# A transformer block on one Trainium2 core: bank order and loads of the first down groups, and sums of squares taken tile by tile

## The chip, the cores and the metric

The kernel runs on one core of one Trainium2 chip. The metric is the device time of one execution in microseconds (us), taken over several runs; a separate execution was profiled, and all rows of a trace come from that one.

## The reference

One encoder block on 512 tokens of width 2048, in float32. Two groups of attention heads (8 grouped-query heads with 2 key/value heads, 8 latent-attention heads, 128 wide each) are each normalised and mapped back by one output projection; then comes a squared-ReLU MLP of width 8192.

```python
o = jnp.concatenate([rms_norm(o_a, g_out_a[l]), rms_norm(o_b, g_out_b[l])], axis=-1)
o = o @ w_out[l]
x = x + gt_a * rms_norm(o, g_post_attn[l])
h = rms_norm(x, g_pre_mlp[l]) * (1.0 + sc_m) + sh_m
y = jnp.square(jax.nn.relu(h @ w_mlp_in[l])) @ w_mlp_out[l]
x = x + gt_m * rms_norm(y, g_post_mlp[l])
```

`gt_a`, `sc_m`, `sh_m` and `gt_m` are parts of `silu(c) @ w_ada + b_ada`.

## The kernel before

Five engines run their own programs and wait on semaphores. Every large product is made three times at reduced precision: a float32 operand is split into a rounded half `hi` (ScalarE, ACT) and a rest `lo` (VectorE, DVE), and TensorE (PE) adds hi x hi, hi x lo and lo x hi in a PSUM bank. Split weights go through a ring of four slots (`RING`), one *unit* at a time: `hi_ready`, `raw_used` or `dn_lo`, and `w_used` count the units that ACT, DVE and PE are done with. SyncE (SP) issues nearly all loads in one order written out by hand, so a wait in SP holds back all loads that stand behind it.

**Output projection** (`out_block`, `out_unit`). Four column blocks of 8 units. A unit is 24 matmuls of 128x512: 4 token tiles `t` by 2 rows `q` by 3. Unit 0 of block 0 lies in the attention of the last head, so `out_block` begins with unit 1 there. The two groups of heads are normalised by their own sums of squares: POOL adds up the squares of each head into `sq_sum`, and `sum_squares` reduces these over the partitions by 12 one-column matmuls with a vector of ones (two instructions each, since they are plain float32) into 8 columns of bank 7. From `sq_reduced` DVE and ACT make `r_out`, which PE waits for ahead of unit 4 of the block (`r_ready`) and behind which ACT splits the weights of units 4 and on; those of units 1 to 3 are split earlier.

**Up stage** (`su_block`). 8 groups of 4 blocks, by a seven-product scheme in place of eight (`SLOTS`). It uses banks 4 to 7. Each block ends in a tile `y_out` that POOL saves to DRAM (`save_pair`, `y_ready`, `y_saved`). Between the blocks DVE adds a row of `w_ada` times a scalar to `gm_acc` (`gate_part`, from `gate_row`, which SP loads in `gate_behind`).

**Down stage** (`dn_products`, `dn_group`, `dn_loads`). 8 groups of rows of the weight, `g`; groups 0 to 6 run in two column halves `np`, and each (g, np) is seven products `i` of two units `h`, 14 units in all, again by the seven-product scheme. A unit is 12 matmuls of 128x512. Product `i` takes the values `y_use[k]`, with k = 0, 1, 2, 3, 4, 6, 5, and the block of weights 11, 12, 11, 22, 22-12 (`diff`), 21, 21, some of them mixed by DVE first (`third`, `one`, `two`, `four`). It writes a pair of banks given by `dn_banks`, and DVE adds the pair to `acc[i]` (`evict`, semaphore `evicted`). The order of DVE around the start of a (g, np) is `third(0)`, `unit_lo(0)`, `third(1)`, `unit_lo(1)`, `one(0)`, `one(1)`, `evict(before, 5)`, `unit_lo(2)`, `two(0)`, `unit_lo(3)`, `two(1)`, `evict(before, 6)`, `unit_lo(4)`. In (0, 0) the last steps of the up stage stand in this order too: behind `unit_lo(2)` comes the last `gate_part` and behind `unit_lo(6)` the last `pair_lo`, which makes `y_ready`.

PE waits for the banks of product i by

```python
wait_dn(pe, evicted, g, np, SLOTS, i - (1 if np == 0 and i < 2 else 2))
```

that is, in column half 0 product 0 waits until product 5 of the group before has been evicted, and product 1 until its product 6 has.

While (0, 1) runs, `spread_gm` multiplies the four column blocks of `gm_acc` by a matrix of ones, in banks 6 and 7, ACT copies each back (`gm_copied`), and POOL adds and multiplies two rows to each. The last group is done another way (`last_products`), 16 units in four column blocks over banks 0 to 3 and 4 to 7.

SP issues the loads at the seam in this order: weights 22, 11 and 12 of (0, 0); values 0 and 1; weights 21; `gate_row`; once the up stage is over values 2, 3 and 4; after `y_ready` values 6; after the last save (`y_saved`) values 5; then the weights 11, 12, 22 and 21 of (0, 1).

Of the kernel before, what the change touches and what calls it, by code (L numbers as in the profile page):

```python
# [26 lines left out]
P = 128  # L27
# [4 lines left out]
COLS = 512  # L32
# [159 lines left out]
def build(nc, a, out, x1_dram, y_dram):  # L192
    with ExitStack() as ctx:
# [336 lines left out]
            return (a_11, s, s, a_12, a_21, a_12, a_22[i % 2])[e]  # L530

        def dn_banks(np, i):
            return 2 * ((SLOTS * np + i) % 3)

        def last_at(n, t):

# [8 lines left out]
        def _(sp):  # L545
# [114 lines left out]
            def gate_behind(g, i):  # L660

                k = 2 * g + (i // 2) if isinstance(g, int) else g * 2 + (i // 2)
                issue = gate_load(k, i % 2)
                if isinstance(g, int) and su_count(g, i, 1) == 0:
                    sp.wait_ge(y_done, 2 * SU_FIRST)
                else:
                    sp.wait_ge(gate_used, su_count(g, i, 1))
                issue()
# [58 lines left out]
            weights(0, 0, "11")  # L727
            weights(0, 0, "12")
            sp.wait_ge(w_used, SU_W + end + 3)
            sp.wait_ge(y_saved, 16 * PAIRS)  # L730
            values(0, 0)
            values(0, 1)
# [1 line left out]
            weights(0, 0, "21", (0,))  # L734
            sp.wait_ge(su_lo, end + 6)
            weights(0, 0, "21", (1,))
            gate_behind(LAST, PAIRS - 1)
            sp.wait_ge(w_used, DN_W)
            for k in (2, 3, 4):
                values(0, k)  # L740
            sp.wait_ge(y_ready, GROUPS * PAIRS)
            values(0, 6)
            sp.wait_ge(y_saved, 16 * GROUPS * PAIRS)
            values(0, 5)
            weights(0, 1, "11")

            def dn_loads(g, np, behind=True):

                def free(n):
                    return lambda: wait_dn(sp, dn_lo, g, np, DN_UNITS, n)  # L750

                def next_values(i):
                    if np:
                        values(g + 1, PRODUCTS[i][1], lambda: sp.wait_ge(w_used, at_dn(g, np, 2 * i + 1).count(1, 1)))

                to = (g + 1, 0) if np else (g, 1)
                weights(*to, "12", free=free(4))
                weights(*to, "22", free=free(8))
                next_values(0)
                next_values(1)  # L760
                next_values(2)
                next_values(3)
                weights(*to, "21", free=free(DN_UNITS))
                if behind:
                    weights(g + 1, np, "11")
                    for i in range(4, SLOTS):
                        next_values(i)
# [3 lines left out]
                n, u = divmod(j, PAIRS)  # L771
                sp.dma_start(last_w[j % LAST_RING][:], w_dn_last[LAST * PAIRS + u, :, :, n * COLS:(n + 1) * COLS]).then_inc(last_landed[j % LAST_RING], 16)

            with sp.Fori(0, LAST - 1) as g:
                dn_loads(g, 0)
                dn_loads(g, 1)
            dn_loads(LAST - 1, 0, behind=False)
# [66 lines left out]
        def _(act):  # L844
# [546 lines left out]
            def final_root(t):  # L1391
                act.wait_ge(y_var, t + 1)
                nc.scalar.activation(stat_s[:, t, 2:3], stat_v[:, t, 2:3], ACT.Sqrt).then_inc(y_sqrt, 1)

            act.wait_ge(x1_saved, 16 * NT)
            plain_blocks()
            su_groups(act, su_block)

            for u in range(2, DN_UNITS):
                unit_hi(0, 0, u)  # L1400
                if u == 2:
                    square_rest(LAST, PAIRS - 1)
                if u == 5:
                    pair_hi(LAST, PAIRS - 1)
            for u in range(DN_UNITS):
                unit_hi(0, 1, u)
                if u >= 7 and u % 2:
                    n = (u - 7) // 2
                    act.wait_ge(gm_reduced, n + 1)
                    nc.scalar.activation(gm_acc[:, n * COLS:(n + 1) * COLS], bank[6 + n % 2][:], ACT.Copy).then_inc(gm_copied, 1)  # L1410
            with act.Fori(1, LAST) as g:
                for np in range(2):
                    for u in range(DN_UNITS):
# [14 lines left out]
        def _(dve):  # L1428
# [868 lines left out]
            def last_evict(n):  # L2297

                dve.wait_ge(w_used, LAST_W + PAIRS * (n + 1))
                for th in range(2):  # L2300
                    b = 4 * (1 - n % 2) + 2 * th
                    dst = acc[((6, 1), (5, 3))[th][n % 2]][:, n // 2, :, :]
                    tt(dst, psum[:, b:b + 2, :], dst, ALU.add).then_inc(last_evicted, 1)

# [8 lines left out]
            def last_tile_sum(t):  # L2313

                dve.wait_ge(last_tile, t + 1)
                y = last_at(NB - 1, t)
                tt(y, bank[t][:], y, ALU.add).then_inc(last_evicted, 1)
                dve.wait_ge(last_evicted, 2 * (NB - 1) + t + 1)
                tt(z_last[:, t, :], y, gm_acc[:, (NB - 1) * COLS:NB * COLS], ALU.mult).then_inc(z_ready, 1)

# [49 lines left out]
        def _(pe):  # L2370
# [280 lines left out]
            def out_unit(n, j, only=range(NT)):  # L2651

                unit_tokens(at_out(n, j)[1], sets[j // 4], o_hi, o_lo, QROWS * out_rows(j), j % 4 == 0, j % 4 == 3, only=only)
# [56 lines left out]
            attend(2 * HEADS - 1, None, stage["v"], HEADS)  # L2710


            def sum_squares():

                pe.wait_ge(sq_ready, 2 * HEADS - 1)
                pe.wait_ge(pt_done, 4 * 2 * HEADS)
                pe.wait_ge(o_done, 2 * HEADS)
                for g in range(2):
                    for t in range(NT):
                        c = 16 + 4 * g + t  # L2720
                        tile = slice(t * P, (t + 1) * P)
                        ins = mm(bank[7][:, c:c + 1], sq_sum[:, g, tile], ones[:, 0:1], start=True, stop=g == 0)
                        if g:
                            ins = mm(bank[7][:, c:c + 1], sq[:, tile], ones[:, 0:1], start=False, stop=True)
                ins.then_inc(sq_reduced, 1)

            def spread_ga(n):

# [5 lines left out]
            def out_block(n, first=False):  # L2734

                for j in range(1 if first else 0, UNITS_D):
                    wait_out(n, j)
                    out_unit(n, j)
                    if j == 1 and first:
                        sum_squares()  # L2740
                    if j == 6:
                        spread_ga(n)

# [121 lines left out]
            def dn_products(g, np, behind=lambda i: None, ahead=lambda i: None):  # L2865

                for i in range(SLOTS):
                    k = PRODUCTS[i][1]
                    b = dn_banks(np, i)
                    ahead(i)  # L2870
                    if np == 0:
                        pe.wait_ge(y_landed[k], g * 16 + 16)
                    wait_dn(pe, evicted, g, np, SLOTS, i - (1 if np == 0 and i < 2 else 2))
                    for h in range(2):
                        w = at_dn(g, np, 2 * i + h)
                        wait_dn(pe, dn_lo, g, np, DN_UNITS, 2 * i + h + 1)
                        s = w.slot()
                        for m in range(2):
                            for q in range(QROWS):
                                j = 2 * h + q  # L2880
                                yh, yl = (y_use[k][:, j, x, m * P:(m + 1) * P] for x in range(2))
                                mm(bank[b + m][:], yh, hi[s][:, q, :], start=j == 0, stop=False)  # L2882
                                mm(bank[b + m][:], yh, lo[s][:, q, :], start=False, stop=False)  # L2883
                                ins = mm(bank[b + m][:], yl, hi[s][:, q, :], start=False, stop=j == PAIRS - 1)  # L2884
                        ins.then_inc(w_used, 1)
                    behind(i)
# [21 lines left out]
            def free_banks(i):  # L2908
# [3 lines left out]
                if i == 2:  # L2912
                    pe.wait_ge(su_c, 3 * SU_BLOCKS)

            def spread_gm(i):

                n = i - 1
                if n == 0:
                    pe.wait_ge(gate_used, SU_BLOCKS)
                    pe.wait_ge(su_x, SU_BLOCKS)  # L2920
                if 0 <= n < NB:
                    if n >= 2:
                        pe.wait_ge(gm_copied, n - 1)
                    mm(bank[6 + n % 2][:], ones[:], gm_acc[:, n * COLS:(n + 1) * COLS], start=True, stop=True).then_inc(gm_reduced, 1)

            dn_products(0, 0, ahead=free_banks)
            dn_products(0, 1, behind=spread_gm)
            with pe.Fori(1, LAST) as g:
                for np in range(2):
                    dn_products(g, np)  # L2930
# [1 line left out]
            def last_products(n, j, t):  # L2932

                s = At(LAST_W + n * PAIRS + j).slot()
                b = 4 * (1 - n % 2) + t
                for q in range(QROWS):
                    yh, yl = (y_use[2 * q + t // 2][:, j, x, (t % 2) * P:(t % 2 + 1) * P] for x in range(2))
                    mm(bank[b][:], yh, hi[s][:, q, :], start=j == 0 and q == 0, stop=False)
                    mm(bank[b][:], yh, lo[s][:, q, :], start=False, stop=False)  # L2939
                    ins = mm(bank[b][:], yl, hi[s][:, q, :], start=False, stop=j == PAIRS - 1 and q == QROWS - 1)  # L2940
                return ins
# [188 lines left out]
```

## Time and profile before

| | |
|---|---|
| runs before | 2078.06 us median of 3 (2077.61 to 2078.45) |
| time of the profiled execution | 2083.07 us |
| its span | 2081.4 us |
| granted TensorE clock, mean over the span | 0.989 |
| PE busy | 2024.3 us (97% of the span) |
| DVE busy | 1717.5 us (83%) |
| ACT busy | 992.1 us (48%) |
| out-projection, from the squares' sums to unit 3 of block 0 | 577.55 to 588.88 us |
| (0, 0) and (0, 1) of the down stage | 1426.56 to 1520.27 us |
| (1, 0) to (6, 1) of the down stage | 1520.27 to 1985.34 us |

Times within a trace count from the start of its span. PE matmuls are pipelined, so the distance from one start to the next, and not the length of a row, is what a matmul costs. The granted clock is the share of TensorE's full clock: 1.00 is 2.4 GHz and 0.50 is 1.2 GHz.

### The profile page before, as it was taken

What the parts mean: (1) busy time and instruction counts of PE and PEld (TensorE: products, weight loads), DVE (VectorE), ACT (ScalarE), POOL (GpSimd) and SP (SyncE); (2) the same over time, 40 slices, a digit from 0 to 9 for tenths busy, and PEclk for the clock granted to TensorE, in tenths of its full rate; (3) what the DMA queues carried; (4) which work ended last, traced back from release to release, by engine and by line L of the source; (5) the groups of instructions that cost most, each with busy time, mean ns of one, the idle gap of its engine ahead of it and who ended that gap; (6) DMA issues with size and microseconds to landing.
All of it is one profiled execution on the core that took longest, in us unless ns stands there. A gap on an engine that the chain in (4) does not pass through costs nothing.

```text
span 2081.4 us, 30860 instructions
## 1 busy us (share of the span) xinstructions
PE 2024.3 (97%) x11186; PEld 1762.0 (85%) x11186; DVE 1717.5 (83%) x2013; ACT 992.1 (48%) x1403; POOL 155.1 (7%) x163
## 2 busy tenths in 40 slices
PE   6999999999999989999999999999999999999998
PEld 6787888878888868899999999998778888888886
DVE  5986898778877777699999999987788888888866
ACT  4454322578833264455565655654333333333322
POOL 0000000057600000000000000000020000000000
PEclk8999999999999999999999999999999999999999
DMA  8996869610186744766667666677756446446452
GB/s 295 344 303 220 280 204 253 200 46 1 54 296 227 241 161 129 247 210 220 224 217 232 212 229 212 218 245 283 258 209 242 181 182 243 181 181 249 174 182 81
DMA packets 296285, 435.37 MB, mean 209 GB/s; under 512 B 30180, under 2 KB 180360, under 8 KB 287368
## 3 DMA queue, kind: packets, MB, share of 16 engines
q1 hardware_dynamic: 278056, 361.43, 52.4%
q0 software_dynamic: 16704, 67.11, 8.8%
q10 hardware_dynamic: 1440, 5.70, 0.8%
q8 instruction: 53, 0.87, 0.2%
q14 instruction: 32, 0.26, 0.0%
HBM read 367.09 MB, written 67.11 MB: 209 GB/s over the span
## 4 chain that ended last, share of the span: by engine, by line
PE 81%; DVE 8%; DMA 4%; issue 3%; ACT 3%; SPq 1%; DVEq 0%; ACTq 0%
PE bank L2860 8%; PE bank L2862 8%; PE bank L2861 8%; PE bank L2882 7%; PE bank L2884 7%; PE bank L2883 7%; PE bank L2384 6%; PE bank L2385 6%; PE bank L2386 6%; PE bank L2397 2%; PE bank L2399 2%; PE bank L2398 2%; DMA raw<-in_w_ada 1%; PE bank L2940 1%; PE bank L2939 1%
## 5 line engine op out<-in xcount | busy, mean ns | idle before, releaser
L2882 PE MATMUL bank<-hi,y_use 128*128 128x512 f32 x784 | 310.2, 396 | 13.9 <-DVE lo L2200 8.5
L1375 ACT ACTIVATE hi<-w 128x1024 fp32r<-128x1024 f32 x168 | 178.1, 1062 | 296.1 <-PE bank L2884 219.9
L2883 PE MATMUL bank<-lo,y_use 128*128 128x512 f32 x784 | 306.6, 391 | 0.0
L2884 PE MATMUL bank<-hi,y_use 128*128 128x512 f32 x784 | 306.6, 391 | 0.0
L851 ACT ACTIVATE hi<-raw 128x1024 fp32r<-128x1024 f32 (+2 forms) x132 | 128.9, 992 | 275.9 <-PE bank L2386 99.6
L1294 ACT ACTIVATE hi<-a 128x1024 fp32r<-128x1024 f32 x182 | 191.9, 1054 | 142.9 <-DVE a L2088 130.4
L2085 DVE TENSOR_TENSOR lo<-a,hi 128x1024 fp32r<-128x1024 f32 x182 | 221.9, 1219 | 40.9 <-ACT hi L1294 40.5
L2200 DVE TENSOR_TENSOR lo<-w,hi 128x1024 fp32r<-128x1024 f32 x168 | 205.2, 1226 | 38.7 <-ACT hi L1375 37.3
L2860 PE MATMUL bank<-h_hi,hi 128*128 128x256 f32 x832 | 235.6, 283 | 0.7 <-DVE c_b L2115 0.7
L2861 PE MATMUL bank<-h_lo,hi 128*128 128x256 f32 x832 | 235.5, 283 | 0.0
L2862 PE MATMUL bank<-h_hi,lo 128*128 128x256 f32 x832 | 235.4, 283 | 0.0
L1436 DVE TENSOR_TENSOR lo<-raw,hi 128x1024 fp32r<-128x1024 f32 (+2 forms) x130 | 147.5, 1141 | 91.8 <-ACT hi L851 89.6
L2882 PEld LDWEIGHTS bank<-hi,y_use 128*128 128x128 f32 x784 | 148.2, 189 | 51.3 <-issue 15.4
L2883 PEld LDWEIGHTS bank<-lo,y_use 128*128 128x128 f32 x784 | 148.3, 189 | 31.3 <-issue 1.0
L2884 PEld LDWEIGHTS bank<-hi,y_use 128*128 128x128 f32 x784 | 148.1, 189 | 31.1
L2860 PEld LDWEIGHTS bank<-h_hi,hi 128*128 128x128 f32 x832 | 159.7, 192 | 0.9 <-DVE c_b L2115 0.9
L2861 PEld LDWEIGHTS bank<-h_lo,hi 128*128 128x128 f32 x832 | 159.7, 192 | 0.0
L2862 PEld LDWEIGHTS bank<-h_hi,lo 128*128 128x128 f32 x832 | 159.7, 192 | 0.0
L2384 PE MATMUL bank<-hi,h_hi 128*128 128x512 f32 x320 | 125.9, 393 | 1.9 <-ACT q_o L1009 1.4
L2088 DVE TENSOR_TENSOR a<-a,a 128x1024 f32<-128x1024 f32 x104 | 124.9, 1221 | 2.4 <-DMA a<-in_w_mlp_in 0.6
L2386 PE MATMUL bank<-hi,h_lo 128*128 128x512 f32 x320 | 124.6, 389 | 0.0
L2385 PE MATMUL bank<-lo,h_hi 128*128 128x512 f32 x320 | 124.6, 389 | 0.0
(384 smaller groups left out, 4715.8 us busy)
## 6 DMA issues: line engine op xcount, KB each, us to landing
raw<-in_w_ada SPq DMA_DIRECT2D x166, 512.0 KB, 5.1
w<-in_w_mlp_out SPq DMA_DIRECT2D x128, 512.0 KB, 4.8
y_dram<-y_out POOLq DMA_DIRECT2D x32, 1792.0 KB, 6.8
y_use<-y_dram SPq DMA_DIRECT2D x53, 1024.0 KB, 9.0
a<-in_w_mlp_in SPq DMA_DIRECT2D x104, 512.0 KB, 4.5
raw<-in_w_in SPq DMA_DIRECT2D x32, 512.0 KB, 5.7
raw<-in_w_out SPq DMA_DIRECT2D x32, 512.0 KB, 4.8
gate_row<-in_w_ada SPq DMA_DIRECT2D x26, 512.0 KB, 5.1
```

The costliest lines, as they stand in the source:

```text
L1294: nc.scalar.activation(hi[w.slot()][:], su_weight(i, e)[:].rearrange("p (q k) n -> p q (k n)", q=QROWS), ACT.Copy).then_inc(hi_ready, 1)
L2085: tt(lo[w.slot()][:], src, hi[w.slot()][:].bitcast(F32), ALU.subtract).then_inc(su_lo, 1)
L2200: tt(lo[w.slot()][:], weight(np, i, h)[:], hi[w.slot()][:].bitcast(F32), ALU.subtract).then_inc(dn_lo, 1)
L2384: mm(acc[t][:], xh, hi[s][:, q, :], start=first and q == 0, stop=False)
L2385: mm(acc[t][:], xh, lo[s][:, q, :], start=False, stop=False)
L2386: ins = mm(acc[t][:], xl, hi[s][:, q, :], start=False, stop=last and q == QROWS - 1)
L2860: mm(into[e], wh, bh, start=opens and k == 0, stop=False, skip_group_check=not opens)
L2861: mm(into[e], wh, bl, start=False, stop=False, skip_group_check=not opens)
L2862: ins = mm(into[e], wl, bh, start=False, stop=k == KH - 1, skip_group_check=not opens)
L2882: mm(bank[b + m][:], yh, hi[s][:, q, :], start=j == 0, stop=False)
L2883: mm(bank[b + m][:], yh, lo[s][:, q, :], start=False, stop=False)
L2884: ins = mm(bank[b + m][:], yl, hi[s][:, q, :], start=False, stop=j == PAIRS - 1)
```

## The change

1. `dn_banks` gives the 14 products of a group four pairs of banks in place of three, in the order 0 1 2 0 1 2 0 | 1 2 3 0 1 2 3, and the wait for evictions is `i - 2` everywhere. The last group's blocks use the other half of the banks (`4 * (n % 2)`).
2. `spread_gm` moves from (0, 1) to (0, 0), behind products 3 to 6, and its copies on ACT move with it; (0, 1) waits for them ahead of product 2.
3. SP loads `gate_row` ahead of values 0 and 1, and the weights 11, 12 and 22 of (0, 1) ahead of values 6 and 5. The first round of `dn_loads` is written out ahead of the loop.
4. `sum_squares` is cut into four parts of 3 matmuls (6 instructions), one for each token tile. They stand behind tiles 2 and 3 of unit 1 and behind tiles 0 and 1 of unit 2.

```diff
         def dn_banks(np, i):
-            return 2 * ((SLOTS * np + i) % 3)
+            return 2 * (0, 1, 2, 0, 1, 2, 0, 1, 2, 3, 0, 1, 2, 3)[SLOTS * np + i]
...
             sp.wait_ge(w_used, SU_W + end + 3)
+            gate_behind(LAST, PAIRS - 1)
             sp.wait_ge(y_saved, 16 * PAIRS)
             values(0, 0)
             values(0, 1)
...
             weights(0, 0, "21", (1,))
-            gate_behind(LAST, PAIRS - 1)
             sp.wait_ge(w_used, DN_W)
             for k in (2, 3, 4):
                 values(0, k)
+            sp.wait_ge(y_done, 2 * GROUPS * PAIRS - 1)
+            weights(0, 1, "11")
+            weights(0, 1, "12", free=lambda: sp.wait_ge(dn_lo, 4))
             sp.wait_ge(y_ready, GROUPS * PAIRS)
             values(0, 6)
+            weights(0, 1, "22", free=lambda: sp.wait_ge(dn_lo, 8))
             sp.wait_ge(y_saved, 16 * GROUPS * PAIRS)
             values(0, 5)
-            weights(0, 1, "11")
...
-                weights(*to, "12", free=free(4))
-                weights(*to, "22", free=free(8))
+                if not begun:
+                    weights(*to, "12", free=free(4))
+                    weights(*to, "22", free=free(8))
...
-            with sp.Fori(0, LAST - 1) as g:
+            dn_loads(0, 0, begun=True)
+            dn_loads(0, 1)
+            with sp.Fori(1, LAST - 1) as g:
...
+                if u in (10, 12):
+                    gate_copy((u - 10) // 2)
             for u in range(DN_UNITS):
                 unit_hi(0, 1, u)
-                if u >= 7 and u % 2:
-                    n = (u - 7) // 2
-                    act.wait_ge(gm_reduced, n + 1)
-                    nc.scalar.activation(gm_acc[:, n * COLS:(n + 1) * COLS], bank[6 + n % 2][:], ACT.Copy).then_inc(gm_copied, 1)
+                if u in (0, 2):
+                    gate_copy(u // 2 + 2)
...
-            def sum_squares():
+            def sum_squares(t):
...
                 for g in range(2):
-                    for t in range(NT):
-                        c = 16 + 4 * g + t
...
+                    c = 16 + 4 * g + t
...
+                if t == NT - 1:
+                    ins.then_inc(sq_reduced, 1)
...
-                    out_unit(n, j)
-                    if j == 1 and first:
-                        sum_squares()
+                    if first and j in (1, 2):
+                        for t in range(NT):
+                            out_unit(n, j, only=(t,))
+                            if j == 1 and t >= 2 or j == 2 and t < 2:
+                                sum_squares(t - 2 if j == 1 else t + 2)
+                    else:
+                        out_unit(n, j)
...
-                    wait_dn(pe, evicted, g, np, SLOTS, i - (1 if np == 0 and i < 2 else 2))
+                    wait_dn(pe, evicted, g, np, SLOTS, i - 2)
...
+            def free_gate_banks(i):
+
+                if i == 2:
+                    pe.wait_ge(gm_copied, NB)
...
-                n = i - 1
+                n = i - 3
...
-            dn_products(0, 0, ahead=free_banks)
-            dn_products(0, 1, behind=spread_gm)
+            dn_products(0, 0, behind=spread_gm, ahead=free_banks)
+            dn_products(0, 1, ahead=free_gate_banks)
...
-                b = 4 * (1 - n % 2) + t
+                b = 4 * (n % 2) + t
```

## Rows read from the trace of the kernel before

**Rows 1.** The page's first part: busy time, share of the span, instructions.
```profile
PE 2024.3 (97%) x11186; PEld 1762.0 (85%) x11186; DVE 1717.5 (83%) x2013; ACT 992.1 (48%) x1403; POOL 155.1 (7%) x163
```

**Rows 2.** PE's waits over the span: total us, times, longest.
```profile
PE bank L2882 <- DVE acc L2280: 3.8, 5, 0.8
```

**Rows 3.** Timeline of PE, down stage: start, length, instruction, [idle before <- releaser].
```profile
1426.56 0.47 PE L2882 MATMUL bank<-hi,y_use 128*128 128x512 f32 x1
...
1434.58 0.39 PE L2884 MATMUL bank<-hi,y_use 128*128 128x512 f32 x1
1439.98 0.80 PE L2882 MATMUL bank<-hi,y_use 128*128 128x512 f32 x1 [5.01 <-DVE lo L2200]
...
1443.66 0.40 PE L2882 MATMUL bank<-hi,y_use 128*128 128x512 f32 x1
...
1475.26 0.77 PE L2882 MATMUL bank<-hi,y_use 128*128 128x512 f32 x1 [3.52 <-DVE lo L2200]
...
1480.52 0.53 PE L2882 MATMUL bank<-hi,y_use 128*128 128x512 f32 x1
...
1489.28 0.80 PE L2882 MATMUL bank<-hi,y_use 128*128 128x512 f32 x1
...
1495.63 0.80 PE L2882 MATMUL bank<-hi,y_use 128*128 128x512 f32 x1
...
1985.34 0.39 PE L2938 MATMUL bank<-hi,y_use 128*128 128x512 f32 x1
```

**Rows 4.** Timeline of DVE at the first two down groups.
```profile
1436.37 1.28 DVE L2123 SCALAR_TENSOR_TENSOR gm_acc<-gate_row,silu_c,gm_acc 128x1024 f32<-128x1024 f32 x1 [5.39 <-DMA gate_row<-in_w_ada]
...
1472.75 1.23 DVE L2204 TENSOR_TENSOR diff<-w,w 128x1024 f32<-128x1024 f32 x1 [8.40 <-issue]
```

**Rows 5.** Timelines of SP's and POOL's queues: values 0, values 2, last save.
```profile
1416.15 0.40 SPq L717 DMA_DIRECT2D y_use<-y_dram  x1
...
1426.47 0.34 SPq L717 DMA_DIRECT2D y_use<-y_dram  x1
...
1447.23 0.94 POOL L3068 DMA_DIRECT2D y_dram<-y_out  x1 [27.25 <-DVE y_out L2042]
```

**Rows 6.** DMA issues, us to landing: values 0, 2, 5; the last saves but one, and last.
```profile
y_use<-y_dram SPq DMA_DIRECT2D x1, 1024.0 KB, 10.3
...
y_use<-y_dram SPq DMA_DIRECT2D x1, 1024.0 KB, 12.4
...
y_use<-y_dram SPq DMA_DIRECT2D x1, 1024.0 KB, 5.0
...
y_dram<-y_out POOLq DMA_DIRECT2D x1, 1792.0 KB, 14.5
...
y_dram<-y_out POOLq DMA_DIRECT2D x1, 1792.0 KB, 10.6
```

**Rows 7.** Windows of 20 us: busy time by engine, PEclk, DMA share, GB/s.
```profile
1420.00:1440.00 20.00, 14.87 (x91) 12.94 (x89) 12.60 (x13) 7.44 (x10) 0.00 (x0) 1.00 1.03 415
```

**Rows 8.** Timeline of PE where groups 3 and 4 begin.
```profile
1674.84 0.39 PE L2884 MATMUL bank<-hi,y_use 128*128 128x512 f32 x1
1675.99 0.49 PE L2882 MATMUL bank<-hi,y_use 128*128 128x512 f32 x1 [0.76 <-DVE acc L2280]
...
1753.56 0.49 PE L2882 MATMUL bank<-hi,y_use 128*128 128x512 f32 x1 [0.77 <-DVE acc L2280]
```

**Rows 9.** Timeline of DVE where group 3 begins.
```profile
1678.05 1.22 DVE L2200 TENSOR_TENSOR lo<-w,hi 128x1024 fp32r<-128x1024 f32 x1
```

**Rows 10.** Timeline of PE around the sums of squares, and a like burst later.
```profile
577.55 1.17 PE L2722 MATMUL bank<-ones,sq_sum 128*128 128x1 f32 x10
...
580.57 0.77 PE L2384 MATMUL bank<-hi,o_hi 128*128 128x512 f32 x1
...
588.88 0.39 PE L2384 MATMUL bank<-hi,o_hi 128*128 128x512 f32 x1
...
734.79 1.84 PE L2770 MATMUL bank<-ones,mod_acc 128*128 128x1 f32 x16
```

More of the change, by code:

```diff
@@ L740, in _, with dn_loads @@
                 values(0, k)
+            sp.wait_ge(y_done, 2 * GROUPS * PAIRS - 1)
+            weights(0, 1, "11")
+            weights(0, 1, "12", free=lambda: sp.wait_ge(dn_lo, 4))
             sp.wait_ge(y_ready, GROUPS * PAIRS)
             values(0, 6)
+            weights(0, 1, "22", free=lambda: sp.wait_ge(dn_lo, 8))
             sp.wait_ge(y_saved, 16 * GROUPS * PAIRS)
             values(0, 5)
-            weights(0, 1, "11")
-            def dn_loads(g, np, behind=True):
+            def dn_loads(g, np, behind=True, begun=False):
                 def free(n):
@@ L1393, in final_root, with gate_copy @@
                 nc.scalar.activation(stat_s[:, t, 2:3], stat_v[:, t, 2:3], ACT.Sqrt).then_inc(y_sqrt, 1)
+            def gate_copy(n):
+                act.wait_ge(gm_reduced, n + 1)
+                nc.scalar.activation(gm_acc[:, n * COLS:(n + 1) * COLS], bank[6 + n % 2][:], ACT.Copy).then_inc(gm_copied, 1)
             act.wait_ge(x1_saved, 16 * NT)
@@ L2300, in last_evict @@
                 for th in range(2):
-                    b = 4 * (1 - n % 2) + 2 * th
+                    b = 4 * (n % 2) + 2 * th
                     dst = acc[((6, 1), (5, 3))[th][n % 2]][:, n // 2, :, :]
@@ L2316, in last_tile_sum @@
                 y = last_at(NB - 1, t)
-                tt(y, bank[t][:], y, ALU.add).then_inc(last_evicted, 1)
+                tt(y, bank[4 + t][:], y, ALU.add).then_inc(last_evicted, 1)
                 dve.wait_ge(last_evicted, 2 * (NB - 1) + t + 1)
@@ L2710, in _ @@
             attend(2 * HEADS - 1, None, stage["v"], HEADS)
-            def sum_squares():
-                pe.wait_ge(sq_ready, 2 * HEADS - 1)
-                pe.wait_ge(pt_done, 4 * 2 * HEADS)
-                pe.wait_ge(o_done, 2 * HEADS)
-                for g in range(2):
-                    for t in range(NT):
-                        c = 16 + 4 * g + t
[L2721 to L2725, printed above, removed]
+            def sum_squares(t):
+                if t == 0:
+                    pe.wait_ge(sq_ready, 2 * HEADS - 1)
+                    pe.wait_ge(pt_done, 4 * 2 * HEADS)
+                    pe.wait_ge(o_done, 2 * HEADS)
+                for g in range(2):
+                    c = 16 + 4 * g + t
+                    tile = slice(t * P, (t + 1) * P)
+                    ins = mm(bank[7][:, c:c + 1], sq_sum[:, g, tile], ones[:, 0:1], start=True, stop=g == 0)
+                    if g:
+                        ins = mm(bank[7][:, c:c + 1], sq[:, tile], ones[:, 0:1], start=False, stop=True)
+                if t == NT - 1:
+                    ins.then_inc(sq_reduced, 1)
             def spread_ga(n):
@@ L2920, in spread_gm @@
                     pe.wait_ge(su_x, SU_BLOCKS)
-                if 0 <= n < NB:
+                if n >= 0:
                     if n >= 2:
```

## The prediction

> **What bounds the kernel now.** First the page's busy times: PE works 97% of the span [rows 1]. So time is to be had only where PE stands still or runs at half clock. I then went through PE's waits by stage. Two stretches are touched by the change.
>
> In the down stage the timeline of PE shows a matmul every 0.227 us (from 1426.56 to 1434.58 there are 35 steps in 8.02 us, of which the first is 0.08 longer than the others), so a unit of 12 takes 2.72 us [rows 3]. From 1426.56 to 1985.34 there are 14 x 14 = 196 units, which would fill 533.1 us; the stage took 558.8. The four gate matmuls explain part of the difference: between the units behind two of them lie 6.35 us in place of 5.44, so 0.91 each, 3.6 in all [rows 3]. The rest is 558.8 - 533.1 - 3.6 = **22.1 us** of standstill and slow clock. It lies in three places:
>
> - PE stops after three units, at 1434.58, and goes on at 1439.98: 5.2 us beyond the usual step. Then nine steps take until 1443.66, 3.7 in place of 2.0: 1.6 lost at half clock [rows 3]. DVE shows why: its last gate_part waited 5.39 us for gate_row, until 1436.37, and two(0) and unit_lo(3) stand behind it in its program [rows 4].
> - PE stops for 3.52 us (3.7 in steps) before 1475.26, the start of (0, 1); then twelve steps take until 1480.52, 5.3 in place of 2.7: 2.5 lost [rows 3]. DVE idled 8.40 us until 1472.75 ahead of third(0), which needs weights 12 and 22 of (0, 1) [rows 4]. SP issued them only after the last save and values 5.
> - At the six starts of groups 1 to 6 PE waits for an eviction [rows 2, 8]. The step there is 1.15 us in place of 0.23, and from one start to the next 77.57 us pass in place of 28 x 2.72 = 76.16: 1.4 each [rows 8]. Six make 8.5, and with the first two places that is 21.5; the last 0.6 is at the seam of groups 0 and 1, where both waits are longer.
>
> In the output projection the squares' sums begin at 577.55, unit 2 at 580.57 and unit 3 at 588.88 [rows 10]. So the sums take 3.0 us, and the 24 matmuls behind them 8.3 in place of 5.44, because the clock fell to its lower level after some 2 us of one-column matmuls.
>
> **The change part by part.**
>
> *Bank order and `i - 2`.* Nothing is added. With four pairs, product 0 of a group waits for product 4 of the one before instead of 5, and product 1 for 5 instead of 6. DVE evicts product 4 even before third(0), so both waits at a group's start go: 8.5 + 0.6 = 9.1 us. What is late next? DVE's run at the start is long: from unit_lo(13) to unit_lo(4) it has 15 operations of 1.1 to 1.2 us with no idle time. Its unit_lo(3) begins at 1678.05 and ends at 1679.3 [rows 9]. PE, started at 1674.84 + 0.23 = 1675.07, wants unit 3 at 1683.2, and the eviction of product 6 (ready at about 1681.5) with product 2 at 1685.9. The slack is 3.9 and 4.4 us, so I take the whole 9.1. Bounds: 7 to 9.1.
>
> *Gate row first.* It is issued at about 1416.2, where values 0 were [rows 5], so it is there long before DVE wants it at 1431, and gate_part costs its 1.28 us and no wait. DVE's chain moves up by 5.39 us, unit_lo(3) is ready at 1439.98 - 5.39 = 1434.6, and PE wants it at 1434.8. Both the 5.2 and the 1.6 us go. But the row's 0.52 MB now stand ahead of values 0, which landed at 1416.15 + 10.3 = 1426.45, just as PE began at 1426.56 [rows 5, 6]: that load is critical already. In that stretch the DMA moved 415 GB/s [rows 7], so 0.52 MB cost 1.3 us; if a save that lands in 14.5 us takes its 127 GB/s of that [rows 6], 1.8. And values 2, whose place in the queue is unchanged in bytes, land at 1426.47 + 12.4 = 1438.9 [rows 5, 6]; PE wants them with unit 4, at 1426.56 + 4 x 2.72 = 1437.4. The old stall hid that. The two delays don't add, since the first moves the second's demand: unit 4 begins at the later of 1437.4 + 1.3 to 1.8 and 1438.9, so at about 1439.0. **New loss 1.6** (bounds 1.5 to 2.7).
>
> *Weights of (0, 1) earlier.* 11 is issued at about 1428, 12 at unit_lo(3), 1434.5, and 22 at unit_lo(7), near 1442.5. Six loads of 0.52 MB behind values 4 are 3.1 MB, or 7.6 us of the DMA. All land by 1457, while third(0) of (0, 1) comes up at about 1460: the 3.7 and 2.5 us go. What is late next is values 6 and 5. y_ready comes 5.4 us earlier, so the last save starts at 1447.23 - 5.4 = 1441.8 [rows 5], but now against a full queue. It took 10.6 us with one load beside it, and the one before 14.5 with a full queue [rows 6]: it lands at 1452.4 to 1456.3. Values 5 take 5.0 more [rows 6], 1457.4 to 1461.3. PE wants them with unit 12: 1439.0 + 8 x 2.72 + 3 x 0.91 = 1463.5. Values 6 (in the queue behind 11 and 12) land near 1455, wanted at 1457.1. So no stall, by a slack of 2 us.
>
> *Gate matmuls in (0, 0).* The same four, 3.6 us as before, moved. Each copy on ACT now waits up to a unit for its matmul, so unit_hi(11), (13), (15) and (17) start about a microsecond after PE leaves the unit whose slot they take. PE wants them three units, 8.2 us, later; hi and lo need 2.3. Cost nothing. POOL's rows move up 40 us and nobody waits for them before the last group.
>
> *Written-out round, banks of the last group.* Same instructions, same waits: nothing.
>
> *Squares tile by tile.* The 24 small instructions stay, 0.107 us each: 2.6 us, and PE pays some 0.1 to get going again after each part, four times in place of once: 3.0 in all. No part is longer than 0.7 us, between stretches of 1.36 us of full matmuls. A burst of 16 such instructions took 1.84 us at 734.79 and the clock stayed at 1.00 [rows 10]; so I expect it to stay here. From 577.55 to unit 3 it was 11.3 us; it becomes 5.44 + 3.0 = 8.4: **2.9 saved** (bounds: 0 or a loss of 0.3, to 2.9). `sq_reduced` comes at 583.2 instead of 580.6. Behind it on DVE and ACT stand the square root and the splits of units 4 and on; unit_lo(4) moves from 584.1 to about 586.5, and PE wants it at 586.0 + 5.4 = 591.4. Hidden.
>
> **Sum.** 22.1 - 1.6 + 2.9 = 23.4 us. From the profiled execution's 2083.07 us that gives 2059.7 (span 2058.0). The median of the runs, 2078.06, is 5.0 lower than the profiled time; it holds the same waits, though perhaps less of them, so I take 23.0 from it: **2055.1 us**.
>
> **Rivals.**
>
> *A. A late load keeps a stall.* The slack of values 5 and 6 is 2 us and rests on how save and loads share the DMA; the first stall (values 0) may be 2.7 us. For: the DMA is full from 1414 to 1442. Against: the old stall was no busier. With a stall of 1 to 3 us and a slow clock behind it (1.6 to 2.5 [rows 3]), it loses 3 to 5 more: 2058 to 2060.
>
> *B. The clock falls anyway.* The one-column parts now alternate with full matmuls over some 6 us, and the clock could fall after any of them. Then the 2.9 are not saved and the additional starts cost 0.3: 2055.1 + 3.2 = 2058.3. Against it stand the burst at 734.79 and the standstills of 0.8 at the groups' starts, which all left the clock at 1.00 [rows 8, 10]. The Trainium skill (TensorE: Matmul & The Clock Gate, HAM oscillation) says that where bursts of matmuls are divided by waits, the clock can fall again at every burst; by that rule spreading could cost more than one block does. The trace bears the rule out for standstills of 3.5 and 5.0 us, and not for short ones.
>
> *C. The bank order does not do what it says.* If another thing of DVE's run is just behind the eviction, the six starts keep their 1.4: 2064. Against: 3.9 us of slack.
>
> *D. Slower than before.* Place: the same run of DVE at the six group starts. If it slipped, PE would stop at unit 3 instead. To eat all 23 us, each start must lose 3.9, so the run must be 3.9 + 3.9 = 7.8 us later than now; that needs each of its 15 operations to take 0.5 longer, 1.7 in place of 1.2 [rows 9]. Nothing in the change lengthens them beyond POOL's eight operations on gm_acc, which lie elsewhere.
>
> **How the numbers follow.** The forecast has 60%, A 20%, B 11%, C 5%, D 2%; 2% is for what I haven't seen, both ways. The range reaches from 2053.0 (no new loss at values 0 and 2, and the last half microsecond of the sum) to 2061.5 (A and B together, less than C). Faster by over 0.2% (4 us, about what a measurement can tell from none): 96%; within it 2%; slower 2%.
>
> **What would show it.** In the trace after: PE goes on at 1434.6 without a stop (times less 2.9 for the projection); DVE's gate_part has no wait; a stop of about 1.5 us in all at values 0 and 2; no stop at the start of (0, 1); no wait for an eviction; 76.2 us from group to group; one-column rows in four parts at full clock. It would be wrong if PE shows a stop of over 2 us anywhere in (0, 0), if unit_lo appears as PE's releaser at the group starts, or if the clock is below 1.00 anywhere from 575 to 590.

## The result and the profile after

| | before | changed |
|---|---|---|
| median of the runs on one chip | 2078.26 us (2077.61 to 2083.28, 4 runs) | 2061.22 us (2057.57 to 2067.83, 4 runs) |
| ratio, 95% interval | | 0.992 [0.9903, 0.9937] |
| profiled execution, its span | 2083.07, 2081.4 us | 2067.83, 2066.1 us |
| mean granted clock in it | 0.989 | 0.989 |

The change makes the kernel faster by 17.0 us between the medians, 16.6 us by the ratio. The forecast was 23.0 us, to 2055.1 us. The median lies inside the range, 0.3 us below its upper end.

The page of the changed kernel has the same instructions as [rows 1], and PE is less busy by 4.7 us:

```profile
PE 2019.6 (98%) x11186; PEld 1762.8 (85%) x11186; DVE 1720.7 (83%) x2013; ACT 992.2 (48%) x1403; POOL 154.8 (7%) x163
```

PE's waits over the span, changed kernel (total us, times, longest). The row of [rows 2] has no counterpart. What is new is a wait in front of a down matmul (L2898) and a longer wait for `lo` in the projection (L2775). `issue` means that the profile names no releaser:

```profile
PE bank L2649 <- DVE pt_lo L1820: 5.2, 6, 1.4
PE bank L2793 <- DVE z_tok L2019: 3.5, 1, 3.5
...
PE bank L2898 <- issue: 2.1, 1, 2.1
PE bank L2775 <- DVE lo L1447: 1.9, 1, 1.9
```

The timeline of PE in the down stage, the answer to [rows 3]. The first rows are the first down unit; 1474.57 is the start of (0, 1), with the last gate matmuls in front of it. Neither the stop behind unit 2 nor the one at (0, 1) is left. The new stop stands in front of the first unit:

```profile
1431.58 0.47 PE L2898 MATMUL bank<-hi,y_use 128*128 128x512 f32 x1 [2.09 <-issue]
...
1432.51 0.63 PE L2898 MATMUL bank<-hi,y_use 128*128 128x512 f32 x1
...
1435.07 0.63 PE L2898 MATMUL bank<-hi,y_use 128*128 128x512 f32 x1
1435.49 0.44 PE L2899 MATMUL bank<-lo,y_use 128*128 128x512 f32 x1
...
1474.12 1.02 PE L2945 MATMUL bank<-gm_acc,ones 128*128 128x512 f32 x2
1474.57 0.80 PE L2898 MATMUL bank<-hi,y_use 128*128 128x512 f32 x1
...
1513.10 0.39 PE L2898 MATMUL bank<-hi,y_use 128*128 128x512 f32 x1
...
1589.26 0.39 PE L2898 MATMUL bank<-hi,y_use 128*128 128x512 f32 x1
...
1970.06 0.39 PE L2959 MATMUL bank<-hi,y_use 128*128 128x512 f32 x1
```

From 1431.58 to 1435.49 there are 10 steps, which take 3.91 us in place of 2.35: the clock was at half for a while. The stop ends with values 0. Their load is issued at 1419.38 and takes 12.1 us in place of the 10.3 in [rows 6], so it lands at 1431.5, and PE goes on at 1431.58:

```profile
y_use<-y_dram SPq DMA_DIRECT2D x1, 1024.0 KB, 12.1
```

1513.10 and 1589.26 are the starts of groups 1 and 2, 76.16 us apart, as 28 units of 2.72 are. DVE's last `gate_part` follows straight on the operation ahead of it, in place of the wait of 5.39 us in [rows 4]:

```profile
1433.94 1.28 DVE L2134 SCALAR_TENSOR_TENSOR gm_acc<-gate_row,silu_c,gm_acc 128x1024 f32<-128x1024 f32 x1
```

SP's queue at the seam (the counterpart of [rows 5]): the gate's row, values 0 and 1, then behind the up stage values 2 to 4, the weights of (0, 1), values 6 and values 5:

```profile
1419.00 0.34 SPq L658 DMA_DIRECT2D gate_row<-in_w_ada  x1
1419.38 0.93 SPq L717 DMA_DIRECT2D y_use<-y_dram  x2
...
1429.52 1.40 SPq L717 DMA_DIRECT2D y_use<-y_dram  x3
1430.97 7.83 SPq L710 DMA_DIRECT2D w<-in_w_mlp_out  x4
1445.23 0.34 SPq L717 DMA_DIRECT2D y_use<-y_dram  x1
...
1458.72 0.34 SPq L717 DMA_DIRECT2D y_use<-y_dram  x1
```

The timeline of PE at the sums of squares, now in four parts (the first two are shown), and at the burst of 16 that [rows 10] has at 734.79:

```profile
576.61 0.50 PE L2733 MATMUL bank<-ones,sq_sum 128*128 128x1 f32 x4
576.98 0.36 PE L2735 MATMUL bank<-ones,sq 128*128 128x1 f32 x2
577.20 0.48 PE L2395 MATMUL bank<-hi,o_hi 128*128 128x512 f32 x1
...
578.67 0.50 PE L2733 MATMUL bank<-ones,sq_sum 128*128 128x1 f32 x4
...
586.19 0.39 PE L2395 MATMUL bank<-hi,o_hi 128*128 128x512 f32 x1
...
731.07 0.50 PE L2775 MATMUL bank<-hi,o_hi 128*128 128x512 f32 x1 [1.93 <-DVE lo L1447]
...
734.37 3.41 PE L2786 MATMUL bank<-ones,mod_acc 128*128 128x1 f32 x16
```

586.19 is the start of unit 3. In the last projection block PE waits 1.93 us for unit 7, and the same burst of 16 then takes 3.41 us in place of 1.84. Windows over the two places tell why. The third number from the end is PE's granted clock, the last two are the DMA's share and GB/s. First the kernel before, then the changed one:

```profile
576.00:592.00 16.00, 16.00 (x70) 13.53 (x69) 10.81 (x17) 7.49 (x10) 1.59 (x3) 0.79 0.91 341
730.00:746.00 16.00, 15.41 (x75) 12.38 (x74) 11.82 (x22) 9.25 (x18) 0.00 (x0) 1.00 0.56 201
```

```profile
576.00:592.00 16.00, 16.00 (x84) 13.65 (x83) 11.33 (x18) 6.98 (x10) 1.60 (x3) 1.00 0.78 291
730.00:746.00 16.00, 14.93 (x50) 11.92 (x51) 8.32 (x13) 5.22 (x11) 0.00 (x0) 0.68 0.47 172
```

The fall of the clock at the sums is gone, and one that costs some 5 us stands behind the wait for unit 7: a mean of 0.68 over 16 us.

To compare all kernels I read the starts of PE's instructions at the borders of three stretches: from the last matmul of the attention to the first transpose of `z_tok` (the projection); from the last matmul of the up stage to the start of (1, 0) (the seam); from there to the last group (groups 1 to 6). From the start of the last group to PE's last matmul it is 86.8 us in each. `Unit 7` is PE's wait for it in the last projection block.

| traced kernel | projection | unit 7 | seam | groups 1 to 6 |
|---|---|---|---|---|
| before, first trace | 182.2 | 0.6 | 94.1 | 465.1 |
| before, again | 180.4 | 1.9 | 93.0 | 464.5 |
| changed, first trace | 185.4 | 1.9 | 83.9 | 457.0 |
| changed, again | 185.6 | 2.2 | 81.8 | 457.0 |
| changed, sums in one block | 183.1 | 2.3 | 82.5 | 457.0 |
| changed, values 0 first | 179.3 | 0.8 | 82.4 | 457.0 |
| before, sums by tiles | 185.9 | 2.3 | 93.6 | 465.3 |
| before, new loads | 178.7 | 0.2 | 82.8 | 464.3 |
| before, new banks | 179.5 | 1.0 | 94.0 | 457.0 |
| values 0 first, unit 4 early | 178.2 | 0 | 82.1 | 457.0 |
| the same, again | 178.2 | 0 | 81.6 | 457.0 |
| the same, sums in one block | 178.2 | 0 | 81.8 | 457.0 |
| before, unit 4 early | 178.2 | 0 | 92.9 | 464.4 |

### The profile page after: what moved, and what is told of

Its sections match the earlier page's. It is cut to its first block, busy times and chain, and to the rows that moved or that the text cites. A ratio compares the mean times of both kernels' runs of the same rounds, so it can differ in the third digit from the quotient of the medians.

```text
span 2066.1 us, 30799 instructions
## 1 busy us (share of the span) xinstructions
PE 2019.6 (98%) x11186; PEld 1762.8 (85%) x11186; DVE 1720.7 (83%) x2013; ACT 992.2 (48%) x1403; POOL 154.8 (7%) x163
## 4 chain that ended last, share of the span: by engine, by line
PE 82%; DVE 6%; DMA 5%; ACT 3%; issue 3%; SPq 0%; DVEq 0%; ACTq 0%
PE bank L2898 9%; PE bank L2900 9%; PE bank L2899 9%; PE bank L2876 8%; PE bank L2877 8%; PE bank L2878 8%; PE bank L2395 4%; PE bank L2397 4%; PE bank L2396 4%; DMA raw<-in_w_out 2%; DMA raw<-in_w_ada 2%; PE bank L2408 2%; PE bank L2410 2%; PE bank L2409 2%; PE bank L2961 1%
## 5 line engine op out<-in xcount | busy, mean ns | idle before, releaser
L2898 PE MATMUL bank<-hi,y_use 128*128 128x512 f32 x784 | 307.7, 393 | 2.1 <-issue 2.1
L1447 DVE TENSOR_TENSOR lo<-raw,hi 128x1024 fp32r<-128x1024 f32 (+2 forms) x130 | 147.6, 1143 | 84.7 <-ACT hi L857 82.1
L2898 PEld LDWEIGHTS bank<-hi,y_use 128*128 128x128 f32 x784 | 147.7, 188 | 33.6 <-issue 3.2
```

## The experiments

Two theories stood at the start. **Theory 1**: the down stage gives what was forecast, and what is missing is the clock of single executions and a later wait in the projection. **Theory 2**: one of the parts costs time of its own, the sums by tiles above all. The first four kernels ran together on one chip, so did the later ones in their groups. Ratios are against the kernel before on the same chip.

**The change again, timed in more runs.** No edit.

> The changed kernel again, for its spread. Four runs of it lie between 2057.6 and 2067.8 us and their mean granted clocks between 0.995 and 0.989. Theory 1, the spread is the clock: in every run the span times the mean clock is the same within 2 us (2043 to 2046 in those four), and the best runs, at 0.995, take about 2057. Theory 2, the spread is in waits for loads: runs of the same clock differ by more than 3 us.

Measured: 2061.36 us (2054.39 to 2064.69, 6 runs), ratio 0.9914 [0.99, 0.9928]. The gain repeats, and so does the gap to the forecast. The runs are 10 us apart, and their mean clocks go from 0.996 (2054.39 us) to 0.992 (2064.69 us). A span times its clock stays within 2043.7 to 2046.5, so most of the spread between runs is the clock; the 2.8 us that stay are a little over the 2 us expected (the clock's third digit is worth 1 us either way). The trace has the wait for unit 7 (2.2 us) with a clock of 0.68 from 730 to 746 again, but a stop of only 1.10 us ahead of the first down unit and no clock fall behind it. Here PE also waits a little ahead of unit 4, for values 2, which land at 1440.87:

```profile
1440.96 0.47 PE L2898 MATMUL bank<-hi,y_use 128*128 128x512 f32 x1 [0.25 <-issue]
```

**The sums in one block, the rest as changed.** `sum_squares` is the whole one again too.

```diff
...
-                    if first and j in (1, 2):
...
-                    else:
-                        out_unit(n, j)
+                    out_unit(n, j)
+                    if j == 1 and first:
+                        sum_squares()
```

> The change with the squares' sums in one block again. If the tile-by-tile sums save their 2.9 us to the end, this is 2.9 slower than the change. If the gain is lost again in the last block of the output projection, where PE now waits 1.9 us for a split weight in place of 0.6 and the clock falls behind it, this is as fast as the change or faster, and its trace shows 0.6 us there and a clock of 1.00 from 732 to 744.

Measured: 2060.9 us (2057.93 to 2065.56, 6 runs), ratio 0.9921 [0.9908, 0.9934]. The medians are 0.5 us apart, not 2.9. But the sign that I had named for a gain lost again, a wait of 0.6 us and a clock of 1.00 there, isn't in the trace either. Its windows show something else: no fall at the sums (1.00), though they are in one block, and a shorter one behind the wait for unit 7 (0.89), which is 2.3 us.

```profile
576.00:592.00 16.00, 16.00 (x85) 13.64 (x84) 11.59 (x18) 7.07 (x10) 1.59 (x3) 1.00 0.89 321
730.00:746.00 16.00, 15.99 (x69) 12.70 (x70) 11.34 (x21) 7.62 (x16) 0.00 (x0) 0.89 0.45 158
```

**Values 0 ahead of the gate's row in SP's queue.**

```diff
-            gate_behind(LAST, PAIRS - 1)
             sp.wait_ge(y_saved, 16 * PAIRS)
             values(0, 0)
+            gate_behind(LAST, PAIRS - 1)
             values(0, 1)
```

> The gate row's load is issued behind values 0 and ahead of values 1. If the 2.1 us stop at the start of the down stage is the 0.5 MB ahead of values 0, the stop goes, so does the slow clock behind it, and what is left is a wait of about 1.5 us for values 2: 0.7 us faster than the change by the stops alone, up to 2.7 with the clock. If values 2 are not what is late next, 2.1 to 4.1 us faster. DVE's gate_part still has no wait by either.

Measured: 2058.71 us (2057.96 to 2059.14, 5 runs), ratio 0.9911 [0.9898, 0.9924]. The stop ahead of the first unit is 0.74 us. A second one of 0.74 is for values 1, which now stand behind the gate's row and land at 1428.81, and one of 0.19 for values 2 follows; all leave the clock at 1.00.

```profile
1428.85 0.50 PE L2898 MATMUL bank<-hi,y_use 128*128 128x512 f32 x1 [0.74 <-DMA y_use<-y_dram]
```

That is 1.7 us of stops in all, where the traces of the change have 2.1 and 1.4: the loss has moved to the next load. The median is 2.6 us lower than that of the change, but the ratios' intervals lie over each other and the seam is no shorter in the table (82.4 against 81.8). So a gain from this order is not shown.

**The sums by tiles alone, on the kernel before.** The diff's part 4.

```diff
...
-                    out_unit(n, j)
-                    if j == 1 and first:
-                        sum_squares()
+                    if first and j in (1, 2):
+                        for t in range(NT):
+                            out_unit(n, j, only=(t,))
+                            if j == 1 and t >= 2 or j == 2 and t < 2:
+                                sum_squares(t - 2 if j == 1 else t + 2)
+                    else:
+                        out_unit(n, j)
```

> The kernel before with the tile-by-tile sums alone. By the sum of the prediction 2.9 us faster than before, by a chain of loads in the last block that takes back what PE gains there 1.5 us faster; not faster or slower where the clock falls at the 16 one-column matmuls behind that wait.

Measured: 2077.74 us (2074.48 to 2084.78, 12 runs), ratio 1.0003 [0.9995, 1.0012]. The 2.9 us don't come. An equal gain would be a ratio of 0.9986, which lies outside the interval. Its trace has the wait for unit 7 (2.3 us) with 0.68 behind it too, so this run alone doesn't tell a gain that is lost again from none.

**The kernel before again, one execution.**

> The kernel before once more, for a second trace. Theory 1, the fall of the clock behind the squares' sums, from which the prediction took 2.9 us, belongs to some executions only: here the clock may stay at 1.00 from 575 to 590, and the stretch from the sums to unit 3 takes 8.4 us in place of 11.3. Theory 2, it comes in every execution: again 0.50 there and 11.3 us. In the last block of the projection PE waits about 2 us for the weights of unit 7, as in the four traces since, and not the 0.6 of the first trace.

Measured: 2079.31 us, span 2077.6 us, clock 0.992. This is the run that shows the mistake. PE's timeline at the sums, and the windows:

```profile
576.91 1.17 PE L2722 MATMUL bank<-ones,sq_sum 128*128 128x1 f32 x10
...
579.51 0.49 PE L2384 MATMUL bank<-hi,o_hi 128*128 128x512 f32 x1
...
585.09 0.39 PE L2384 MATMUL bank<-hi,o_hi 128*128 128x512 f32 x1
```

```profile
576.00:592.00 16.00, 16.00 (x84) 13.67 (x83) 11.82 (x18) 7.09 (x10) 1.60 (x3) 1.00 0.93 342
730.00:746.00 16.00, 16.00 (x77) 13.20 (x78) 12.44 (x23) 9.26 (x18) 0.00 (x0) 1.00 0.47 171
```

The same kernel, the same block of 24 instructions: from the first of them to unit 3 (585.09) it is 8.18 us, where [rows 10] has 11.33. The clock didn't fall. The 24 small instructions take 2.60 us (576.91 to 579.51), where the first trace has 3.02. The wait for unit 7 is 1.9 us in this trace and 0.6 in the first.

**The new loads alone, on the kernel before.** The diff's part 3.

> The kernel before with the new order of loads alone. Both stops at the seam go (5.2 and 3.7 us) and a stop of 1.5 to 2.5 at values 0 comes: 6.5 to 7.5 us faster by the stops, up to 11 where the clock would have fallen. The six waits of 0.8 for evictions at the groups' starts stay.

Measured: 2069.22 us (2066.49 to 2070.94, 5 runs), ratio 0.9952 [0.9939, 0.9966]: some 10 us. The seam goes from 93.0 to 82.8 us, and the five short waits for evictions stay as in [rows 2]. The new stop at values 0 is 1.2 us, less than the 1.5 to 2.5 expected:

```profile
PE bank L2888 <- DVE acc L2286: 3.8, 5, 0.8
PE bank L2888 <- issue: 1.2, 1, 1.2
```

**The new banks and the gate matmuls in (0, 0) alone, with the old loads.** The diff's parts 1 and 2.

> The kernel before with the new order of banks and the gate matmuls in (0, 0) alone. The six groups' starts lose no time, 76.2 us from group to group: 8 to 9 us faster. The stops of 5.0 and 3.5 at the seam stay. With the loads alone it adds up to the change; if it does not, the two meet somewhere.

Measured: 2072.85 us (2067.71 to 2073.66, 6 runs), ratio 0.9966 [0.9952, 0.998]: some 7 us. Groups 1 to 6 take 457.0 us in place of 464.5, and the seam is no shorter (94.0). Its two stops stay, 4.8 us behind unit 2 and 2.7 ahead of (0, 1), with three short waits behind them:

```profile
PE bank L2887 <- DVE lo L2205: 9.8, 5, 4.8
```

The two halves are 0.48% and 0.34%; together they make the 0.8% of the change, which leaves nothing for the sums. The intervals are 0.14% wide to each side, as much as the 2.9 us, so this sum alone doesn't decide it.

**Unit 4 split early.** The wait for unit 7 comes from the ring. ACT's program has the squares of block 2 (L1190) ahead of its split of the last block's unit 4, so the slot comes free late, SP loads late (720.70 and 723.15), and the last halves are made when PE wants them. ACT in the changed kernel:

```profile
715.55 0.63 ACT L1190 ACTIVATE part<-part 128x512 f32<-128x512 f32 x1 [11.14 <-DVE z_tok L1953]
...
718.35 2.01 ACT L857 ACTIVATE hi<-raw 128x1024 fp32r<-128x1024 f32 x2 [0.23 <-ACT part L1190]
724.46 1.06 ACT L857 ACTIVATE hi<-raw 128x1024 fp32r<-128x1024 f32 x1 [4.10 <-DMA raw<-in_w_out]
728.63 1.06 ACT L857 ACTIVATE hi<-raw 128x1024 fp32r<-128x1024 f32 x1 [3.11 <-DMA raw<-in_w_out]
```

The edit, on the kernel with values 0 first:

```diff
+            out_his(0, range(4, 5))
             with act.Fori(0, NB - 1) as n:
-                out_his(n, range(4, 8))
+                out_his(n, range(5, 8))
                 a_part(n)
-                for j in range(4):
+                for j in range(5):
                     split_hi(at_out(n, j)[0].plus(OUT_RAW_N), at_out(n, j)[1].plus(OUT_W_N))
...
-            out_his(NB - 1, range(4, 8))
+            out_his(NB - 1, range(5, 8))
```

> The change with values 0 ahead of the gate row, and ACT's split of unit 4 of each projection block ahead of the squares of the block before. If PE's wait of about 2 us for unit 7 in the last block comes from ACT splitting unit 4 so late that the load into its place in the ring is late too, the wait goes, and the fall of the clock behind it with it: 2 us faster than the change with values first, up to 5. If the load itself is slow whenever it is issued, the wait stays and it is the same.

Measured: 2057.11 us (2056.44 to 2059.16, 4 runs), ratio 0.9897 [0.9882, 0.9912], the lowest median of all, though its interval overlaps that of the kernel with values 0 first (0.9911 [0.9898, 0.9924]). PE has no wait for unit 7 any more and the projection takes 178.2 us.

**The same again, and with the sums in one block, side by side.**

> The same kernel as the one that gave 2057.1 us (values 0 first, unit 4 split early, sums tile by tile), again, beside the one with whole sums on the same chip. Both theories: 2056 to 2059 us.

> The version with values 0 loaded first and the split of unit 4 ahead of the squares of the block before (2057.1 us), but with the squares summed in one block of 64 as in the kernel before. Theory 1: once PE no longer waits for unit 7, the 2.9 us that the tile-wise sums save ahead of unit 3 come through to the stop at z_tok; whole sums then cost about 2.9 us: 2060.0 us. Theory 2: the order of the sums is worth nothing in any setting, because a later wait (at z_tok, 3.5 to 3.9 us) takes it back: 2057.1 us, within 1 us of the run with tile-wise sums on the same chip.

Measured: by tiles 2057.77 us (2056.99 to 2058.12, 4 runs), ratio 0.9902 [0.9887, 0.9917]; in one block 2057.55 us (2056.49 to 2061.28, 4 runs), ratio 0.9906 [0.989, 0.9921]. My theory 1 of this pair falls: with the wait for unit 7 gone, the sums by tiles still give nothing. The ratios alone could hide 2.9 us; what decides is that the projection takes 178.2 us in both. Windows of the kernel with the sums in one block, then of the one with tiles:

```profile
576.00:592.00 16.00, 16.00 (x85) 13.64 (x84) 11.54 (x18) 6.73 (x9) 1.59 (x3) 1.00 0.91 341
730.00:746.00 16.00, 16.00 (x80) 13.56 (x79) 13.45 (x29) 10.51 (x23) 0.00 (x0) 1.00 0.37 152
```

```profile
576.00:592.00 16.00, 16.00 (x81) 13.49 (x81) 9.64 (x15) 6.20 (x8) 1.60 (x3) 1.00 0.78 282
730.00:746.00 16.00, 16.00 (x78) 13.48 (x78) 13.62 (x29) 10.95 (x23) 0.00 (x0) 1.00 0.35 142
```

It isn't that the gain is made and lost again, for here nothing could take it (178.2 us for the projection in both). There is no gain to be made unless the clock falls at the block. In one block the sums and unit 2 take 8.18 us; counted from the same place (one tile, 1.36 us, earlier) that is 9.54, and by tiles it is 9.58 (576.61 to 586.19 in the changed kernel).

**The early split of unit 4 alone, on the kernel before.** The edit of above.

> The kernel before with one edit alone: the split of unit 4 of each projection block ahead of the squares of the block before; nothing of the change. Theory 1: the wait for unit 7 (0.6 to 1.9 us in two traces of the kernel before) goes and the projection ends that much earlier: 1 to 2 us faster than the kernel before, ratio 0.999 to 0.9995. Theory 2, unit 7 bounds PE only where the sums are made tile by tile: no difference, ratio 1.000.

Measured: 2076.77 us (2074.22 to 2079.03, 11 runs), ratio 0.9996 [0.9987, 1.0005]. Its trace has no wait for unit 7 and 178.2 us for the projection, 2.2 us less than the second trace of the kernel before. (It is 4.0 less than the first, of which some 3.2 is the slow clock at the sums.) In the times a gain of 1 to 2 us can't be told from none, so this run decides nothing.

## Why the prediction was right and where it was wrong

**The down stage was right in its steps.** `gate_part` has no wait; PE goes on behind unit 2 without a stop; (0, 1) begins without one; no wait for an eviction is left at a group's start. Group to group it is 76.16 us, as forecast, and groups 1 to 6 take 457.0 us in all eight traces with the new banks. Seam and groups together were 559.2 us in the first trace; less 22.1 and with the new 1.6 that is 538.7, and the traces of the changed kernels whose clock doesn't fall there have 538.6 to 539.5. Rival C falls, and D with it. Rival A's late values 5 and 6 don't show in the three traces with the change's own order of loads. (The kernel with the new loads alone, which has no gate matmuls in (0, 0), waits 0.2 us for values 6.)

**The new loss at values 0 was forecast at 1.6 us (1.5 to 2.7).** The gate's row ahead of values 0 does make PE stop there: 2.09 us with half clock behind it in the first trace, 1.10 in the second, 2.36 in the one with the sums in one block, the last two without a clock fall. The 36 steps of the first three units take 9.9 us in the first trace in place of 8.3, so 1.6 more are slow clock, and that trace lost 3.7 us there. My bound "a stop of over 2 us in (0, 0)" was crossed, by the mechanism named. Values 2 are late only behind the shortest of the three stops, by 0.25 us; the longer ones cover them. In the two traces without a clock fall the stops come to 1.35 and 2.36 us, where the bounds were 1.5 and 2.7. That the clock can fall behind this stop stood in rival A and not in the term.

**The step that failed is "2.9 saved" for the squares tile by tile.** The prediction read 11.3 us from the sums to unit 3 in one execution, and took the 3 us that came from the lower clock as what a block of one-column matmuls costs each time. Seven traces have the sums in one block. In one of them, the one that I had, the clock fell at its end (0.79 from 576 to 592); in the other six it stayed at 1.00 and the stretch takes 8.17 to 8.18 us. By tiles the clock stays at 1.00 as well, as forecast, and the stretch comes to the same to 0.04 us; the 0.1 that I put down for each start of a part isn't there either. So the term is 0 in place of 2.9, inside the bounds that I gave and taken at the wrong end. The times agree: 1.0003 for the sums alone, 0.9914 against 0.9921 and 0.9902 against 0.9906 with the rest. The 3.0 us that I read for the sums themselves held 0.4 of slow clock too: they take 2.60 without it. The row that spoke against the term stood in my own [rows 10]: 16 such instructions at 734.79 had left the clock alone. I used it for the parts, and not against the block. Rival B was the same error turned round: I asked whether the clock would fall in the changed kernel, and not whether it would fall again in the one before. The Trainium skill (TensorE: Matmul & The Clock Gate, HAM oscillation) has the clock fall where waits divide bursts; the four parts, with full matmuls and no waits between them, show none in six traces. Why the clock fell at the block in that one execution no run shows, nor whether the parts make such a fall rarer: 0 of 6 traces against 1 of 7 is no difference.

**The second failure is the base of the sum.** The first trace of before spent 94.1 us on the seam and 465.1 on groups 1 to 6; the second 93.0 and 464.5. So 1.7 of the 20.5 us that I forecast for the down stage is there in one execution and not in the other. Between the second traces of the two kernels, the seam and the groups give 11.2 + 7.5 = 18.7 us. The prediction took 0.4 off its 23.4 for "perhaps less" of the waits in the median runs, though a profiled time 5.0 us above the median already said that its waits and clock falls were more than usual.

**What is left of the gap.** 23.4 less 2.9 and less 1.8 is 18.7; measured were 17.0 between the medians, 16.6 (13.1 to 20.2) by the ratio. The 18.7 lie inside that interval, so there may be nothing left to explain. A rest of some 2 us would fit the wait for unit 7, which the prediction did not have: it is 1.9 to 2.3 us in both traces of the change, in the one with its sums in one block and in the one with the sums by tiles alone, and in all four 2 to 5 us are lost to half clock behind it. But this wait is in the kernel before too, and it varies between traces (0.6 and 1.9 us), so that it costs the change something that it doesn't cost the kernel before is argued, not shown. Its length (0.2 to 2.3 us without the early split) is set ahead of the load, which takes 5.2 to 5.8 us in each of these traces. ACT's squares of block 2 wait for DVE's `z_tok`. In the eight traces of this kind without slow clock at the sums they begin 141.3 to 142.1 us behind the last matmul of the attention where the wait is 0.2 to 1.0 us, and 143.2 to 144.1 behind it where it is 1.9 to 2.3. What makes DVE later in one execution than in another stays open.

**The upper end of the range.** It was said to hold rivals A and B together, but 2061.5 has room for 3.2 us each; with the 5 us that A names at most it would have been 2063.3. That the median lies inside was luck in part: the sums' term and the base missed to the same side, and the range was made for other causes.

## What to carry to other kernels

Before a term is read off one trace as "matmuls took longer here", ask whether it is standstill or slow clock, and whether a second trace shows it again. The waits for evictions came back in every trace with the old banks (3.8 us in five waits); the wait for unit 7 came back with 0.2 to 2.3 us; the slow clock at the sums did not come back in six. If the profiled time lies above the median, look for the episodes that make up the difference, and take them out of what the edit is to save. And when a stall goes, follow the buffer ring one use further: here one split, moved ahead of another stage's work in ACT's program, takes a wait away in every trace at no cost that shows, though its gain is too small to be told from none in the times.

## What the runs showed that was not expected

The same kernel has its clock falls in different places in different executions. Before: from 579.7 to 586.5, and not at all there in the second trace. The stretch from 730 to 746, behind a wait of about 2 us and ahead of 16 one-column matmuls: 0.68 in three traces (waits of 1.9, 2.2 and 2.3 us), 0.89 in one (2.3 us), 1.00 in one (1.9 us, the kernel before) and 1.00 in all with a wait under 1.1 us. With the two ahead of the first down unit (2.1 and 2.4 us) these are seven stops of 1.9 to 2.4 us, and five have half clock behind them. The longest has none. So such a stop may cost its own length, or more than three times that, in one and the same kernel. The ten stops of 2.7 to 5.0 us at the seam, in the five traces with the old loads, all have half clock behind them. So has the stop of 3.5 to 3.9 us for `z_tok` in each of the thirteen traces, but in four of these (the first two of the change among them) the clock had fallen before that stop began, behind two waits of 1.0 and 0.9 us.
